# Attention scores of the next unit in two parts on TensorE, around the turning of the weights

## The reference

```python
def diff_attention(q, k, v, p, lambda_init):
    H, d = DIFF_HEADS, DIFF_QK_DIM          # 4 heads, two components of 64
    ...
    lam = jnp.exp(jnp.sum(lam_v[0] * lam_v[1])) - jnp.exp(jnp.sum(lam_v[2] * lam_v[3])) + lambda_init

    def attend(qb):
        s = jnp.einsum('bqhcd,bkhcd->bhcqk', qb, k)
        pr = jax.nn.softmax(s, axis=-1)
        amap = pr[:, :, 0] - lam * pr[:, :, 1]
        return jnp.einsum('bhqk,bkhe->bqhe', amap, v)
```

## Time and profile before

| | us |
|---|---|
| median of three runs | 2192.07 |
| lowest and highest | 2185.35, 2193.34 |
| the profiled execution | 2197.07 |
| its span, first to last instruction | 2194.5 |
| attention stage, first score to last product | 650 to 927 |

### The profile page before, as it was taken

The page is one execution under the profiler, slowest core; times in us unless marked ns, Lnnn a source line. Parts: engine busy times, 40 slices in busy tenths (PEclk is TensorE's granted clock), DMA queues, the critical chain, the costliest instruction groups (busy, mean ns, idle before and its releaser), DMA issues. The chain is left out here.

```text
span 2194.5 us, 40752 instructions
## 1 busy us (share of the span) xinstructions
PE 1997.5 (91%) x16199; PEld 1665.3 (76%) x16199; DVE 1411.1 (64%) x2299; ACT 969.5 (44%) x1792; POOL 349.1 (16%) x354
## 2 busy tenths in 40 slices
PE   6999999997768888777999698899999999999999
PEld 4666777775545555576887387899999999988887
DVE  5877657674876667664777646656655565556666
ACT  7454467773744444443454322422232232333433
POOL 0000000000019993064454200000000000000000
PEclk8999999998879999958999899899999999999999
DMA  4111157777840001047884534022222222295343
GB/s 179 66 45 52 58 206 258 257 261 278 288 136 1 0 1 58 20 125 166 195 187 117 174 127 141 35 100 93 105 81 87 81 100 81 84 356 169 98 148 109
DMA packets 153305, 281.17 MB, mean 128 GB/s; under 512 B 13377, under 2 KB 85953, under 8 KB 150817
## 3 DMA queue, kind: packets, MB, share of 16 engines
q1 hardware_dynamic: 153120, 278.63, 39.8%
HBM read 172.53 MB, written 103.07 MB: 126 GB/s over the span
## 5 line engine op out<-in xcount | busy, mean ns | idle before, releaser
L2944 DVE TENSOR_TENSOR ff_lefts<-normed_raw,ff_lefts 128x512 fp32r<-128x512 f32 x154 | 105.5, 686 | 98.6 <-ACT ff_lefts L2828 98.6
L225 PE MATMUL ff_acc<-right_t_high,ff_lefts 128*128 128x320 f32 x528 | 163.1, 309 | 0.0
L224 PE MATMUL ff_acc<-right_t_low,ff_lefts 128*128 128x320 f32 x528 | 163.1, 309 | 0.0
L223 PE MATMUL ff_acc<-right_t_high,ff_lefts 128*128 128x320 f32 x528 | 163.1, 309 | 0.0
L223 PE MATMUL ff_acc<-normed_nl 128*128 128x512 f32 x385 | 149.8, 389 | 0.0
L225 PE MATMUL ff_acc<-normed_nl,normed_nh 128*128 128x512 f32 x385 | 149.8, 389 | 0.0
L2828 ACT CAST ff_lefts<-normed_raw 128x512 fp32r<-128x512 f32 x154 | 93.4, 620 | 116.2 <-DMA normed_raw<-in_w_up 56.1
L2854 ACT COPY normed_n<-ff_acc 128x640 f32<-128x640 f32 x66 | 45.9, 696 | 205.7 <-PE ff_acc L225 204.6
L1974 PE MATMUL at_pO<-heads_vt,at_amT 128*128 128x128 f32 (+1 forms) x624 | 104.6, 302 | 34.9 <-ACT at_amT L1918 24.5
L1974 PEld LDWEIGHTS at_pO<-heads_vt,at_amT 128*128 128x128 f32 (+1 forms) x624 | 82.8, 195 | 61.0 <-issue 40.0
L3016 DVE TENSOR_TENSOR normed_nl<-normed_raw,normed_nh 128x640 fp32r<-128x640 f32 x77 | 63.3, 822 | 91.7 <-ACT normed_nh L2877 91.7
(11 more groups left out here) (372 smaller groups left out, 5671.9 us busy)
## 6 DMA issues: line engine op xcount, KB each, us to landing
normed_raw<-dram_h SPq DMA_DIRECT2D x77, 320.0 KB, 3.0
ch_ops<-dram_sx SPq DMA_DIRECT2D x88, 256.0 KB, 5.2
dram_sx<-pr_sx SPq DMA_DIRECT2D x16, 1024.0 KB, 4.6
dram_h<-normed_spread_h SPq DMA_DIRECT2D x44, 320.0 KB, 2.3
pj_packed<-in_w_in SPq DMA_DIRECT2D x24, 512.0 KB, 4.9
heads_vt<-dram_ab SPq DMA_DIRECT2D x44, 256.0 KB, 5.4
normed_raw<-in_w_gate SPq DMA_DIRECT2D x22, 512.0 KB, 4.3
normed_raw<-in_w_up SPq DMA_DIRECT2D x22, 512.0 KB
```

The source lines that it names most:

```text
L223: nc.tensor.matmul(out, ll, rh, start=start, stop=False, skip_group_check=onto_kept)
L224: nc.tensor.matmul(out, lh, rl, start=False, stop=False, skip_group_check=onto_kept)
L225: return nc.tensor.matmul(out, lh, rh, start=False, stop=stop, skip_group_check=onto_kept)
L2944: tt(lefts[:, q % LEFTS, 1, :], raw[:, y, QUARTER[p], :], lefts[:, q % LEFTS, 0, :].bitcast(F32), ALU.subtract).then_inc(low, 1)
```

## The change

`score` takes a second argument. Part 0 holds the two waits for the exponentials and the first piece of keys (512, or all 272 of a short unit), part 1 the pieces behind it (512 and 16 keys; nothing in a short unit). The signal `scores[x]` still stands behind the last piece. In the loop, part 0 stays where the scores were, and part 1 comes behind `turn(k - 1, 0)` and ahead of `times_v(k - 1, 0)`.

```diff
-                def score(k):
+                def score(k, part):
                     h, q0, a, ln, v0 = units[k]
-                    for x in range(2):
-                        pe.wait_ge(exped[x], PRIMED + k)
-                    for lo in range(0, ln, 512):
+                    if part == 0:
+                        for x in range(2):
+                            pe.wait_ge(exped[x], PRIMED + k)
+                    for lo in range(0, ln, 512)[part:1 if part == 0 else None]:
                         hi = min(lo + 512, ln)
...
-                score(0)
+                for part in range(2):
+                    score(0, part)
                 pe.wait_ge(ident_in, PRIMED + 16)
                 for k in range(1, ALL + 1):
                     if k < ALL:
-                        score(k)
+                        score(k, 0)
                     if k:
                         turn(k - 1, 0)
+                        if k < ALL:
+                            score(k, 1)
                         times_v(k - 1, 0)
```

## The result

The changed kernel takes 2235.14 us (median of four runs, 2233.88 to 2236.97), the kernel before 2192.70 (four runs). The ratio is 1.019 with a 95% interval of 1.017 to 1.021: **slower by 42 us**, where 16 had been forecast and 2221 was the upper end of the range. The sign was right, the size was not.

What follows compares the result with a forecast made beforehand. Attention was taken as bound by waits around TensorE's holes, no engine being full. Long periods add 11.7 us and heads' edges 4.7, together 16.4 over the median 2192.07, giving 2208.5 us; range 2195 to 2221.

Steps and rivals of the forecast that it cites:

- Where the time is: In long attention periods TensorE's hole of 0.77 closes; one of 1.43 opens ahead of batch 1's turning, awaiting the exponential.
- Rival 3: Batch 1's turning has room on its wait for the exponential, so the covered copy counts: faster, 2181 us; chance 0.05.
- The last score: Scores end later by the turning between their parts: 0.42 of weight loads plus 0.20 fixed, 0.62 us.
- Two stretches have it twice: A stretch of scores has a fixed part of 0.20 us, so splitting it in two adds 0.20.
- The period, uncontended: A full-clock long period without GpSimd contention grows from 7.08 to 7.42 us, 0.34 longer.
- The loop through VectorE: Slack of VectorE's difference before the first turning drops from 1.43 to 0.17; under GpSimd's work periods are 7.61, 0.53 longer.
- Edges of the heads: Around short units and a head's first and last long units, later scores and waits for the difference add 4.7 us.
- Rival 2: TensorE's clock falls for one more long period per head, at the heads' edges: 4 x 3.7 us more, 2223; chance 0.12.

Runs made afterwards that it cites:

- run 3: Changed kernel with row maxima over the first 512 keys only, the rest left out; 2203.90 us (one execution).
- run 4: Kernel before with row maxima over the first 512 keys only, the rest left out; 2193.61 us (one execution).
- run 2: Changed kernel with scores split behind 1024 keys in place of 512, so only the last 16 keys follow the turning; 2217.45 us, ratio 1.010.
- run 6: Changed kernel without GpSimd's triangular solve, its inverses left zero; 2225.50 us (one execution).
- run 7: Kernel before without GpSimd's triangular solve, its inverses left zero; 2194.36 us (one execution).
- run 1: Changed kernel with five more 128x128 products adding zeros on TensorE, in the hole ahead of batch 1's turning; 2228.61 us, ratio 1.017.
- Run 11: Changed kernel with two zero-adding products on TensorE behind batch 2's turning; 2223.11 us, ratio 1.014.
- 5: Kernel before with one more ScalarE copy (128x384) ahead of the copy of batch 0 in long units; 2211.87 us, ratio 1.007.
- 9: Kernel before with one more ScalarE copy (128x512) ahead of the copy of batch 0; 2202.61 us (one execution).
- 10: Kernel before with two more ScalarE copies (128x384 each) ahead of the copy of batch 0; 2225.61 us (one execution).

## Why the prediction was right in sign and wrong in size

- **Where the time is.** Right. The hole ahead of batch 0's products closed (24.5 us of waits to 3.1) and a longer one opened ahead of batch 1's turning, released by the exponential. Rival 3 is ruled out: run 3 shows that path to be the one that counts, and shows it by moving it. One ground given against rival 3, that batch 1's turning waited already 25 times, did not hold: by run 4 that wait of 0.17 cost nothing in the kernel before.
- **The last score.** Mis-sized: 0.62 forecast, 2.93 - 2.14 = 0.79 measured. The step that failed is "Two stretches have it twice": the 0.20 of the second stretch is there (1.06 and 1.19 against 2.04 in one), but behind the transposes stands another 0.17 of idle weight load, in the rows of every period. The Trainium skill (TensorEngine Tiling (Array Packing), Key Properties) has each change of tiling mode drain the engine. The rows agree, with 0.17 ahead of the second stretch and 0.20 in it, though no run tells a drain from another cause; the split makes two such changes, and only the 0.20 was in the sum.
- **The period, uncontended.** 7.42 forecast, 7.54 measured, 0.46 in place of 0.34 over 7.08. Run 2 has the same 7.54 from the late last score alone. By this term the sum would have been some 3 us higher (25 x 0.12).
- **The loop through VectorE.** Right in mechanism: TensorE's own waits for the difference ahead of the first turning went from 3.8 us in 3 to 8.6 in 13, without GpSimd's work (run 6) the contended periods are gone, and run 7 shows that this work had been free before. In size it was about right: 17 periods were put at 0.19 beyond the uncontended one, 3.2 us. The six seen in the middle of the changed kernel's heads hold 2.4, some of them with a part of a clock's fall, and the seven of run 1, all at full clock, 2.9.
- **Edges of the heads.** 4.7 forecast; run 2, in which nothing else is disturbed, has 3.0 in the first long units and 2.0 towards the short ones, so 5.0. But the long unit behind a head's first one, largely at half clock, had been put at nothing in three heads of four; over all four it has 3.0 in run 2 and 5.4 in the changed kernel. How much of that the change made is open: these four units took 39.0 us in the kernel before and 35.1 in run 7, the same order without GpSimd's work, as the half clock there lasted longer or shorter. The last unit's 3.7, by its clock of 0.74, had no term either.
- **TensorE's clock.** Rival 2 had the right cause of over half of what was missing, 13.6 of the 23.7 us between the forecast's 16.4 and the stage's 40.1, and for the most part the wrong place. It was priced as one half-clock period more per head, at the head's edge, 15 us, with a chance of 0.12. That its price comes near is partly luck. Measured were nine slow periods: two by a half clock that lasted longer from the head's edge, 3.4 us, as rival 2 has it, and seven by new falls in the middle of heads, 10.2 us. Run 11, without either kind, is 12 us faster than the changed kernel. The step that failed is the ground given against it, "holes of 0.77 in each period of 7.08 left the full clock alone": it was read as leave for a hole of 1.43, and it says nothing on an order that splits the scores. The runs showed in its place that a hole of 1.27 in the split order goes with seven new falls in 23 periods, while 0.82 (run 11) and 0.72 (run 3) in the same order go with none. Runs 5, 9 and 10 would have misled too, since in the unsplit order even 1.53 is harmless.

What stays open is why the clock falls. Shown, with one profiled execution each: it falls in the changed order, with GpSimd's work and without (run 6); filling the hole with two products or shortening it to 0.72 (run 3) stops it, and so does a split 0.86 us later with the hole in two parts; and in the unsplit order neither the hole's length nor its place brings more than one slow period in 23. So it fell again and again only where the split order and a hole of over 0.82 came together. What of the split order matters, the transposes between the scores or something else, was not tried.

## What to carry to other kernels

Work that is ready can fill a hole only at the price of what stands behind it: before moving it, find what waits for its last instruction, here the maximum and the exponential, and what it now waits for itself. A wait in a trace does not prove a path: the 0.17 before the turning cost nothing, and only cutting the maxima showed it. And shortening the wait that ends a hole (a copy in two halves with a signal each) gained 0.22 a period, where moving work into the hole lost 0.46.

## What the runs showed of the hardware

- Transposes between two stretches of scores cost 0.20 for the second stretch and 0.17 of idle weight load ahead of it, beside their own 0.42.
- The granted clock, at 2.4 GHz in the middle of heads, fell to 1.2 GHz there seven times in the 23 periods of the changed kernel, with a hole of 1.27, never with a hole of 0.72 or 0.82 in the same order (runs 3 and 11), and once in all runs of the unsplit order, even with holes of up to 1.53. A slow period took 1.3 to 1.7 us more than 7.54.
- VectorE's difference of a long unit took 1.30 us in all 32 units without GpSimd's work and up to 2.11 beside it in the kernel before.
- In the kernel before the time at half clock at the heads' edges differs between executions: 10.77 us was one such unit in its trace, 8.59 the same unit in run 7.
- One ScalarE copy of 128x512 took 0.59 us and two of 128x256 took 0.37 and 0.38, started 0.27 apart: against the turning the pair ends 0.06 later than the whole copy did, and the products start 0.22 sooner.
